# Light expert units loaded two heavy blocks behind their place on TensorE, and eight heavy blocks to a light stage

## The reference

```python
def _moe(h, router, w_gate, w_up, w_down):          # h (1, 256, 1024)
    logits = (xf @ router).astype(jnp.float32)
    top_logits, top_idx = lax.top_k(logits, 2)
    gates = jax.nn.softmax(top_logits, axis=-1)
    ...
    def run_block(args):
        tok, e = args
        return _swiglu(x_pad[tok], w_gate[e], w_up[e], w_down[e])   # (silu(x Wg) * (x Wu)) Wd
    ...
    out = jax.ops.segment_sum(y, slot_tok, num_segments=N + 1)[:N]
```

## Time and profile before

| | before |
|---|---|
| median of three runs | 1515.26 us |
| the profiled execution: its time, its span | 1516.86 us, 1515.0 us |
| mean granted TensorE clock | 0.998 of full speed |
| TensorE busy | 1476.6 us (97%) |
| VectorE, ScalarE busy | 911.1 us (60%), 734.3 us (48%) |
| first light matmul, last light matmul | 684.65 us, 1422.5 us |
| DMA over the span | 469.61 MB |

### The profile page before, as it was taken

One profiled execution on the slowest core, in us unless ns is written; L12 is line 12 of the kernel. 1 busy time (PEld: TensorE's weight loads), 2 busy tenths in 40 slices (PEclk: granted clock), 3 DMA queues, 4 the chain that ended last, 5 costly groups with the idle time before them and its releaser, 6 DMA issues.

```text
span 1515.0 us, 22445 instructions
## 1 busy us (share of the span) xinstructions
PE 1476.6 (97%) x9550; PEld 1133.6 (75%) x9550; DVE 911.1 (60%) x665; ACT 734.3 (48%) x588; POOL 302.9 (20%) x295
## 2 busy tenths in 40 slices
PE   9999999999999999999999999999999999999997
PEld 8887889999998878886666666667666666666785
DVE  6555665655556866885555546555555555555686
ACT  5444455344336435774444445444444544444565
POOL 5599324500024401880000000000000000000100
PEclk9999999999999999999999999999999999999999
DMA  9645538765531164999999999999999999999993
GB/s 346 190 161 173 172 134 299 276 232 190 182 129 42 47 259 150 374 392 407 394 410 403 398 409 413 411 408 408 407 401 397 410 402 409 407 394 407 409 396 150
DMA packets 141597, 469.61 MB, mean 310 GB/s; under 512 B 8648, under 2 KB 21152, under 8 KB 129200
## 3 DMA queue, kind: packets, MB, share of 16 engines
q1 hardware_dynamic: 137424, 454.58, 78.3%
q0 software_dynamic: 3920, 13.44, 2.7%
q10 hardware_dynamic: 144, 0.07, 0.0%
HBM read 462.02 MB, written 15.21 MB: 315 GB/s over the span
## 4 chain that ended last, share of the span: by engine, by line
PE 73%; DMA 14%; DVE 6%; ACT 4%; issue 1%; POOL 1%; POOLq 0%; SPq 0%; ACTq 0%; DVEq 0%
PE PS L2066 70%; DMA weights_raw<-in_moe_w_up 8%; DVE weights_lo L1560 4%; DMA weights_raw<-in_moe_w_gate 4%; ACT weights_hi L1132 3%; PE PS L2281 1%; DMA row_back<-results_by_slot,pair_index 1%; DMA weights_raw<-in_moe_w_down 1%; POOL b_padded L950 1%; PE PS L2480 1%; ACT c_padded L1132 0%; DMA results_by_slot<-small_expert_rows 0%; DVE residual L1560 0%; DMA constants<-in_constants 0%; DVE residual L1955 0%
## 5 line engine op out<-in xcount | busy, mean ns | idle before, releaser
L1560 DVE TENSOR_TENSOR weights_lo<-weights_raw,weights_hi 128x2048 fp32r<-128x2048 f32 (+2 forms) x323 | 680.2, 2117 | 406.4 <-ACT weights_hi L1132 405.3
L1132 ACT ACTIVATE weights_hi<-weights_raw 128x2048 fp32r<-128x2048 f32 (+2 forms) x323 | 564.7, 1754 | 465.2 <-PE PS L2066 311.2
L2066 PE MATMUL PS<-weights_hi,gathered_hi 128*128 128x512 f32 (+1 forms) x640 | 240.2, 375 | 1.6 <-DVE weights_lo L1560 1.0
L2066 PE MATMUL PS<-weights_hi,gathered_lo 128*128 128x512 f32 (+1 forms) x640 | 234.5, 366 | 0.0
L2066 PE MATMUL PS<-weights_lo,gathered_hi 128*128 128x512 f32 (+1 forms) x640 | 234.2, 366 | 0.0
L2066 PE MATMUL PS<-weights_hi,act_transposed_hi 128*128 128x512 f32 x456 | 185.9, 408 | 2.3 <-DVE weights_lo L1560 2.3
L2066 PE MATMUL PS<-x_transposed_hi,weights_hi 128*128 128x256 f32 x640 | 181.2, 283 | 1.3 <-DVE weights_lo L1560 1.1
L2066 PE MATMUL PS<-weights_hi,act_transposed_lo 128*128 128x512 f32 x456 | 180.6, 396 | 0.0
L2066 PE MATMUL PS<-weights_lo,act_transposed_hi 128*128 128x512 f32 x456 | 180.0, 395 | 0.0
L2066 PE MATMUL PS<-x_transposed_hi,weights_lo 128*128 128x256 f32 x640 | 179.6, 281 | 0.0
L2066 PE MATMUL PS<-x_transposed_lo,weights_hi 128*128 128x256 f32 x640 | 179.6, 281 | 0.0
(11 more groups left out here) (330 smaller groups left out, 1453.4 us busy)
## 6 DMA issues: line engine op xcount, KB each, us to landing
weights_raw<-in_moe_w_up SPq DMA_DIRECT2D x127, 896.0 KB, 9.7
weights_raw<-in_moe_w_gate SPq DMA_DIRECT2D x125, 896.0 KB, 9.6
weights_raw<-in_moe_w_down SPq DMA_DIRECT2D x96, 1024.0 KB, 8.3
weights_raw<-in_ret_w_in SPq DMA_DIRECT2D x24, 1024.0 KB, 6.6
weights_raw<-in_moe_w_down SPq DMA_DIRECT2D x32, 512.0 KB, 9.0
weights_raw<-in_ffn_w_gate SPq DMA_DIRECT2D x14, 1024.0 KB, 5.1
weights_raw<-in_ffn_w_up SPq DMA_DIRECT2D x14, 1024.0 KB, 5.1
weights_raw<-in_ffn_w_down SPq DMA_DIRECT2D x14, 1024.0 KB, 4.9
```

The source lines that it names most:

```text
L1132: return nc.scalar.activation(o, i, ACT.Copy)
L1560: return nc.vector.tensor_tensor(o, a, b, op)
L2066: return nc.tensor.matmul(o, l, r, start=start, stop=stop)
```

## The change

The lag of the light loads (`behind`) goes from 1 to 2. A light stage of six blocks is spread over 8 heavy blocks each time, where it was 7 and 8 in turn. The four `add_back` steps stand at units 36, 38, 40 and 42 of the last heavy expert, where they stood at 30, 33, 36 and 39.

```diff
     for stage in range(len(LIGHT) * ESTEPS):
         for at in range(6):
             after[k] = 6 * stage + at
-            k += 2 if at == 3 else 1
-        k += stage % 2
+            k += 2 if at in (3, 5) else 1
     return after
...
-ORDER = units_in_order(1)
+ORDER = units_in_order(2)
 USED_ORDER = units_in_order(0)
...
-                        if q == LAST and i in (30, 33, 36, 39):
-                            add_back(0, (i - 30) // 6, (i - 30) // 3 % 2)
+                        if q == LAST and i in (36, 38, 40, 42):
+                            add_back(0, (i - 36) // 4, (i - 36) // 2 % 2)
```

## The result

The changed kernel takes 1927.14 us (median of 4 runs, 1920.54 to 1931.81). The kernel before takes 1516.08 us beside it (4 runs, 1514.31 to 1519.34). The ratio is 1.2705, with a 95% interval of 1.2661 to 1.2749. The profiled execution took 1927.55 us with a span of 1925.8. The forecast was 1850, with a range up to 1915: the time lies 12 us above the range.

What follows compares the result with a forecast made beforehand. It took TensorE (97% busy) and, while expert weights stream, full DMA engines as the joint bound. 1736 + 48.5 + 11.6 + 12 = 1808 us, plus 43 for the clock, gave about 1850, 80% in 1780 to 1915.

Steps and rivals of the forecast that it cites:

- The loop: Expert stretch: light unit, heavy unit, split, then next light second unit's load wait on each other; 71 steps, 1043 us.
- close steps: The 48 steps pairing one heavy and one light block; each forecast at 13.35 us where its bytes need 9.0.
- the signs of the loop: Light silus 88 to 92 us apart, DMA 270 to 300 GB/s, PE about 70% busy, some 48 waits of 4 to 5 us.
- far steps: The 23 steps with a heavy block between; two light units follow the heavy load closing the loop, 17.5 us each.
- The landing: Time for the loop's 896 KB load to arrive with nothing queued ahead: 4.75 us, bounds 2.2 to 9.0.
- The spreading and the adds: After the last light block: nine heavy blocks 48.5 us, the first add's stall 12 us, the tail 11.6 us.
- The stall at the first add: VectorE waits at the first `add_back` for gathered rows, holding up later splits and PE: 12 us.
- the clock's term: TensorE's clock falls in half of the 48 close-step waits, at 1.8 us each: 43 us.
- the last light block's end: Loop start at 691.4, plus 1043 us of steps and 1.8 us: 1736 us, without the clock.
- The start: The loop begins when the split for the first moved light load begins, as before: 691.4 us.
- The rival that the clock falls at nearly every wait: Close-step waits nearly all lower the clock, 48 x 3 us = 144 us: about 1950 us, chance 0.07.
- the forecast of 1808: Span of the whole kernel if the clock holds and each matmul costs what it did: 1808 us.

Runs made afterwards that it cites:

- e1: The changed kernel with the lag of the light loads back at one heavy block; even spacing and later adds stay: 1536.84 us.
- e2: The kernel before with a lag of two heavy blocks and nothing else changed: 1946.53 us.
- e5: The changed kernel with VectorE writing only a quarter of `weights_lo` from the 70th expert unit on, the rest stale: 1823.98 us.
- e6: The kernel before with VectorE writing only a quarter of `weights_lo` from the 70th expert unit on, the rest stale: 1508.2 us.
- e3: The changed kernel with 14 or 30 small extra matmuls ahead of light units, meant to fill PE's waits: 1961.76 us.
- e7: The changed kernel with fewer small extra matmuls, 8 or 16 to a place, nearer to PE's long waits: 1900.98 us.
- e4: The changed kernel with light loads three units behind their place, one heavy unit sooner than its four: 1647.38 us.
- e9: The changed kernel at a three-unit lag, with the light stage's ScalarE and VectorE work one heavy unit later, behind the split: 1610.4 us.

## Why the prediction was off, step by step

**The loop: right in its length, and in about half of the close steps in its place.** Each link that was forecast is in the chain in its order, and e1 and e2 put 390 of 411 us on the lag. e5 and e6 test it from the side: a shorter split is worth 103 us in the loop and 10 outside. The silus came out 98 us apart rather than 88 to 92; the DMA rate of 269 GB/s, PE's 76% and the waits of 4.6 to 4.9 us are near what was named as the signs of the loop. 90 waits came, not some 48, since many steps have a wait of 1 or 2 us beside the long one, and far steps wait too.

**The landing: right.** 4.7 us against my 4.75, with nothing ahead in the queue; the estimate of 4.1 us by the Trainium skill ("DMA: Bandwidth & Descriptors", section "Anatomy of one DMA — SWDGE (gpsimd) path") would have been short by 0.6, as the kernel before's row already said.

**The spreading and the adds: right within 1 us in sum.** From the end of the last light block to the end of the span I had 48.5 + 12 + 11.6 = 72.1 us; it is 1925.8 - 1852.7 = 73.1. The stall at the first add, 12 forecast, is 10.6; the nine heavy blocks took some 2 us longer than forecast, of which a part is the low clock behind that stall (the first matmul there took 0.76 us).

**Where it failed: the clock's term, "I take half of the 48 at 1.8 us each: 43 us".** All of the miss lies ahead of the last light block's end, 1852.7 where 1736 was forecast without the clock. That is 117 us, and the term had 43. PE's timeline gives each of the 71 steps, from the start of one light block's second unit to that of the next. The 48 close ones took 14.7 us on average, where 13.35 was forecast, and the 23 far ones 19.6, where 17.5 was: 65 and 48 us in sum.

How much of this is the clock can be estimated from the same trace. I take each piece of PE's work in the chain of waits and multiply it by what the granted clock lacked there (0.5 where it was 0.50). That gives 59 us in the close steps, 1.24 each, and 42 us in the far ones, 1.83 each; with the last light unit it is 104 us. Without it a close step is 13.5 us long and a far one 17.7, so the links of the loop were right within 0.3 us a step, 11 us in sum. The start came 1.5 us later than forecast.

So the term was too small in two places. The larger is the far steps: the term has nothing for them, and gives no reason. The sum has them as 17.5 us of loop like any other, and PE waits there 3.4 to 6.3 us for the first unit of each light gate stage, which then begins at the low clock, as in the row at 1086.11. The other is the close steps, 59 us where I had 43. There I took half of the waits, but of the 56 light units that PE waited for by 3 us or more 55 met the low clock. And the loss doesn't end with the light unit, which loses 3.25 - 1.72 = 1.5 us: behind the wait of 1816.67 the heavy unit's first two matmuls took 0.80 and 0.63 us, and 0.50 and 0.40 in the heavy unit at 1805.23.

The rival that the clock falls at nearly every wait, to which I had given 0.07, names what happened. Its price did not: 48 x 3 = 144 us, all at close steps. That its 1950 is nearer to 1927 than my 1850 is in part luck. Against it I had held that PE runs for over 8 us on end in each step and should have its clock back; it has it back, and loses it again in the next wait. This is as the Trainium skill has it in "TensorE: Matmul & The Clock Gate", section "HAM oscillation — how this bites in real kernels", that a kernel waiting for a load at each tile starts every tile on the halved clock. The trace agrees but for one unit in 56, with 3.25 us for a unit behind a wait and 1.72 for one without.

The growth of PE's busy time, 131 us, is more than these 104. By the same estimate the whole execution has 127 us of low clock in PE's work, of which 106 lie in the chain; the other 20 or so filled time in which PE would have waited in any case. That the idle time of 317.9 us is near the 331.4 which the forecast of 1808 implies (1808 - 1476.6) is for this reason no test of the loop.

The 104 us take the chain as it is. That they would all come back with a full clock is not shown: less work between two waits could also mean a longer wait. e3 and e7 took 97 and 91 us off PE's own work, but their added matmuls lay on the path for 133 and 56, so they show only that the low clock costs time.

One reading of the prediction was off as well, without effect on the sum: by the 0.71 of the first window in the earlier trace rows the clock fell at 1510.4, 3.4 us after PE stopped and not 3.7.

**A second step, unforeseen and small in the sum: the order of ScalarE's program.** I had the wait of each close step ahead of the second light unit. A wait of 3 us or more stands there in 23 of the 48, and ahead of the *first* unit in 21. In 11 of these 21 the split that frees the slot for the first unit stands in ScalarE's program behind the silu of the light stage, as at 1106.79 above; in 4 it stands behind the copy of the heavy expert's transposed activations, in 5 behind copies of gathered rows or a heavy silu. So what e4 showed at three units is in the changed kernel too. The steps' mean length shows that it cost little: that loop is closed over other links, but it is about as long.

What of e4's loss is left in e9, 74 us over e1, is explained in part only. The rows say that PE waits for loads. In 10 of the 18 waits of 1.2 us or more ahead of a light unit the split that freed the slot stood behind another copy in ScalarE's program (gathered rows, transposed activations), which e9 left where they were. No run moved these.

## What to carry to other kernels

A load that is issued in order into a ring of slots inherits the wait of whatever frees its slot; before its place in the queue is moved, name for each load which use frees its slot, and check that this use doesn't stand behind the very consumer that wants the previous load of that kind. Follow it also through the order of the engines' own programs: e4 kept the buffers free and closed the loop over a silu in front of a split. And when a loop makes TensorE stop for some us in each step, as here, price the work behind the stop at the low clock in every step of every kind, and count only the part that lies on the chain.

## What the runs showed of the hardware

The clock also fell where PE's idle time was split into short pieces. PE's timeline of e5:

```profile
1107.93 1.72 PE L2067 MATMUL PS<-weights_raw,small_gathered 128*64 128x448 f32 x8 [1.13 <-DMA weights_raw<-in_moe_w_up]
1111.75 3.25 PE L2067 MATMUL PS<-weights_raw,small_gathered 128*64 128x448 f32 x8 [2.10 <-DMA weights_raw<-in_moe_w_up]
```

The second unit runs at the low clock behind idle times of 1.13 and 2.10 us with a unit of 1.72, at the full clock, between them. I had thought of one long piece as what brings the clock down, and so expected e5 to win up to 110 us of clock; it won 46 us of busy time. Keeping the array at work with matmuls is no free remedy: 8 and 16 of them to a place gave 26 us of 411, and 14 and 30 cost 35, because part of them fell where TensorE wasn't waiting.
